# Splitting eight small reads between two DMA queues and moving one inverse root on VectorE

## The reference

```python
q = l2_normalize(qkv[..., :A_KEY_W].reshape(bsz, s, A_HEADS, A_DK)) * (A_DK ** -0.5)
a_mat = jnp.where(strict, jnp.einsum("bhncd,bhnsd->bhncs", k_beta, k) * decay, 0.0)
sol = lax.linalg.triangular_solve(a_mat + jnp.eye(CHUNK, dtype=f32), rhs, left_side=True, lower=True, unit_diagonal=True)
```

## Time and profile before

| | us |
|---|---|
| median of 3 runs | 952.58 |
| lowest, highest | 951.58, 954.92 |
| the profiled execution's own time | 954.44 |
| its span, first to last instruction | 952.6 |
| PE busy, of the span | 925.1 (97%) |
| DVE busy | 610.0 (64%) |
| ACT busy | 497.1 (52%) |

### The profile page before, as it was taken

One profiled execution on the slowest core, in us unless ns is written; L12 is line 12 of the kernel. 1 busy time (PEld: TensorE's weight loads), 2 busy tenths in 40 slices (PEclk: granted clock), 3 DMA queues, 4 the chain that ended last, 5 costly groups with the idle time before them and its releaser, 6 DMA issues.

```text
span 952.6 us, 13974 instructions
## 1 busy us (share of the span) xinstructions
PE 925.1 (97%) x5264; PEld 786.6 (83%) x5264; DVE 610.0 (64%) x1037; ACT 497.1 (52%) x867; POOL 31.1 (3%) x43
## 2 busy tenths in 40 slices
PE   5999989999999999899999999999999999999998
PEld 5899989799989898677888888887776788888886
DVE  4787967776566687867654454546887665554443
ACT  4478342464566576666544444535586654444431
POOL 1001000000000012100000000010000000000000
PEclk9999989999999999999999999999999999999999
DMA  9454331356533545314555655555444266555550
GB/s 327 139 174 145 96 104 45 111 183 218 175 134 133 162 146 196 110 45 133 178 176 178 191 192 188 177 177 174 140 132 134 92 198 191 181 176 179 183 190 22
DMA packets 106293, 148.22 MB, mean 156 GB/s; under 512 B 12564, under 2 KB 59344, under 8 KB 106112
## 3 DMA queue, kind: packets, MB, share of 16 engines
q1 hardware_dynamic: 102014, 145.34, 47.2%
q0 software_dynamic: 704, 1.77, 0.5%
q10 hardware_dynamic: 3522, 0.39, 0.3%
HBM read 146.03 MB, written 1.45 MB: 155 GB/s over the span
## 4 chain that ended last, share of the span: by engine, by line
PE 87%; DVE 7%; ACT 3%; issue 1%; DMA 1%; ACTq 0%; SPq 0%; DVEq 0%
PE ps L1879 25%; PE ps L1881 24%; PE ps L1880 24%; PE ps L1974 4%; DVE wlo L1159 3%; ACT whi L641 1%; PE ps L2111 1%; PE ps L2105 1%; PE ps L2259 1%; DVE G L1324 1%; PE ps L2467 0%; PE ps L2498 0%; DMA C<-in_consts 0%; PE ps L2046 0%; PE ps L2065 0%
## 5 line engine op out<-in xcount | busy, mean ns | idle before, releaser
L1159 DVE TENSOR_TENSOR wlo<-raw,whi 128x1024 fp32r<-128x1024 f32 (+1 forms) x272 | 321.3, 1222 | 213.4 <-ACT whi L641 213.1
L641 ACT ACTIVATE whi<-raw 128x1024 fp32r<-128x1024 f32 (+1 forms) x272 | 271.2, 1045 | 270.9 <-PE ps L1881 270.7
L1879 PE MATMUL ps<-whi,xh 128*128 128x512 f32 (+1 forms) x544 | 217.7, 400 | 1.3 <-DVE wlo L1159 1.0
L1881 PE MATMUL ps<-whi,xl 128*128 128x512 f32 (+1 forms) x544 | 211.9, 389 | 0.0
L1880 PE MATMUL ps<-wlo,xh 128*128 128x512 f32 (+1 forms) x544 | 211.5, 389 | 0.0
L1879 PEld LDWEIGHTS ps<-whi,xh 128*128 128x128 f32 x544 | 102.2, 188 | 23.1 <-issue 3.4
L1881 PEld LDWEIGHTS ps<-whi,xl 128*128 128x128 f32 x544 | 102.1, 188 | 21.4
L1880 PEld LDWEIGHTS ps<-wlo,xh 128*128 128x128 f32 x544 | 102.4, 188 | 18.6
L1879 PE MATMUL ps<-xh,whi 128*128 128x256 f32 x384 | 112.5, 293 | 3.3 <-DVE xl L1225 3.0
L1880 PE MATMUL ps<-xl,whi 128*128 128x256 f32 x384 | 109.6, 285 | 0.0
L1881 PE MATMUL ps<-xh,wlo 128*128 128x256 f32 x384 | 109.5, 285 | 0.0
(11 more groups left out here) (391 smaller groups left out, 1178.1 us busy)
## 6 DMA issues: line engine op xcount, KB each, us to landing
raw<-in_l_w_gate SPq DMA_DIRECT2D x44, 512.0 KB, 3.9
raw<-in_l_w_up SPq DMA_DIRECT2D x44, 512.0 KB, 4.9
raw<-in_l_w_down SPq DMA_DIRECT2D x44, 512.0 KB, 4.6
raw<-in_l_w_in SPq DMA_DIRECT2D x36, 512.0 KB, 4.5
raw<-in_a_w_in SPq DMA_DIRECT2D x32, 512.0 KB, 4.7
raw<-in_w_kv SPq DMA_DIRECT2D x16, 512.0 KB, 4.9
raw<-in_b_w_in SPq DMA_DIRECT2D x16, 512.0 KB, 4.4
raw<-in_l_w_o SPq DMA_DIRECT2D x16, 512.0 KB, 4.3
```

The costliest lines, as they stand in the source:

```text
L641: nc.scalar.activation(whi[:, g % HIGH, a], raw[:, g % RAW, a], ACT.Copy).then_inc(hi_done, 1)
L1159: nc.vector.tensor_tensor(wlo[:, g % LOW, a], raw[:, g % RAW, a], whi[:, g % HIGH, a].bitcast(F32), ALU.subtract).then_inc(lo_done, 1)
L1879: mm(o_, a_h, b_h, start=start, stop=False, skip_group_check=True)
L1881: return mm(o_, a_l, b_h, start=False, stop=stop, skip_group_check=True)
```

## The change

Two edits. On DVE the inverse root of the queries and its scaling move out of slot 43 into the first level of the joining, between the masks of the second and third quarters. The PSUM read stays in slot 43. The keys' root stays where it was. On the Y side SP issues four of the eight reads, and ACT the other four, in slot 54 (`CONV_V - 1`), behind the same waits as SP. The number of DMAs and the counts on `blocks` stay the same.

```diff
                     with nc.allow_non_contiguous_dma(reason="diagonal blocks of 16 by 16"):
-                        for b in range(NB):
+                        for b in range(NB // 2):
                             sp.dma_start(diagonal_block(Y, b), blocks_y[b].rearrange("n i j -> i n j")).then_inc(S("blocks"), 16)
...
+                if s == CONV_V - 1:
+                    act.wait_ge(S("inv_zero"), 2)
+                    act.wait_ge(S("blocks"), 16 * NB + 32)
+                    with nc.allow_non_contiguous_dma(reason="diagonal blocks of 16 by 16"):
+                        for b in range(NB // 2, NB):
+                            act.dma_start(diagonal_block(xn[:].rearrange("p t n -> p (t n)"), b),
+                                          blocks_y[b].rearrange("n i j -> i n j")).then_inc(S("blocks"), 16)
                 if s == CONV_V:
                     act.wait_ge(S("solved"), 1)
                     act.dma_start(blocks_x.rearrange("b n i j -> (b n) (i j)"), blk_x).then_inc(S("x_blocks"), 16)
...
             def summed(name, n):
 
-                ms, y, t = rms[name]
                 dve.wait_ge(S("col_sum"), n + 1)
-                nc.vector.tensor_scalar(by_stat(ms), stat_ps, 1.0, EPS, ALU.mult, ALU.add).then_inc(S("stat_read"), 1)
+                nc.vector.tensor_scalar(by_stat(rms[name][0]), stat_ps, 1.0, EPS, ALU.mult, ALU.add).then_inc(S("stat_read"), 1)
+
+            def rooted(name, n):
+
                 dve.wait_ge(S("stat_read"), n + 1)
-                inverse_root(ms, y, t).then_inc(step(name, "root"), 1)
+                inverse_root(*rms[name]).then_inc(step(name, "root"), 1)
                 dve.wait_ge(*past(name, "root", 1))
...
                 if s == COL_SUM_AT[0]:
                     summed("k", 0)
+                    rooted("k", 0)
...
                 if s == COL_SUM_AT[1] + 2:
                     summed("q", 1)
-                    link(nc.vector.tensor_scalar(rq, rq, float(P) ** -0.5, None, ALU.mult))
...
             for lv in range(3):
                 for q_ in range(4):
                     a = slice(512 * q_, 512 * q_ + 512)
+                    if lv == 0 and q_ == 2:
+                        rooted("q", 1)
+                        link(nc.vector.tensor_scalar(rq, rq, float(P) ** -0.5, None, ALU.mult))
                     dve.wait_ge(S("t2"), 4 * lv + q_ + 1)
```

## The result

The changed kernel took 956.38 us in the median of 20 runs (955.0 to 960.0), the kernel before 952.71 us in the median of 20 (951.58 to 955.36). The ratio is 1.0037, with a 95% interval of 1.0029 to 1.0045: slower by 3.5 us, by the ratio. The forecast was that nothing changes, 952.6 us with a range up to 955.4, and the measured time lies above that range. Rival B, given 8%, had said 956.7 us.

The account below looks back on a forecast made before the run. PE was taken to be bound by the chain through ACT's eight X-read issues and the silu, not by the Y reads. The terms 0 + 0 + 0 + 0 + 0 gave 0 us: 952.6 us, range 950.4 to 955.4.

Parts of the forecast that it names:

- Rival B: The blocks_x write stands behind the weight loads: 2.8 us later plus 1.3 us of clock, together 4.1 us, 956.7 us; chance 8%.
- The write of `blocks_x`: ACT's write, issued at 118.69 without slack, now behind 1 MB of weights: delay between 0 and 2.8 us, taken as 0.
- rival A: PE's clock stays up in t2, 1.8 us, and its 1.53 us gap goes: 949.3 us; chance 6%, clock alone 6%.
- the low part of unit 12: On DVE, without the root in slot 43, it runs 1.8 us earlier, from about 100.5; no gain in itself.
- that of unit 13: On DVE, unit 13's low part can start at 106.2 instead of 106.84, limited by its first high half.
- the solve's end: The rest of the solve comes 0.6 us earlier, L529 at 114.4 instead of 115.00; worth 0.
- ACT's four issues in its idle time: ACT's four added reads in slot 54 run from 116.2 to about 118.1, within its 5.18 us idle; cost 0.
- the loads at 118.13: SP's weight transfers, issued at 120.65 before, go out at about 118.1 after four fewer reads; gain 0.
- `t2` at 120.31: PE starts t2 at 120.5 as the Y reads land sooner and the 1.53 us wait goes; gain 0.
- the new gap behind its first quarter: PE's gap moves behind t2's first quarter, ended by the L809 copies at 123.16; later work starts as before, gain 0.
- the root hidden under PE's wait: The root's 2.3 us on DVE fit in its 4.38 us wait before the third quarter's mask; cost 0.
- Rival C: ACT's new issues overrun slot 54 if two queues double the 0.48 us issue: 1.4 us later, 954.0 us; chance 5%.

Follow-up runs that it names:

- just_behind: Changed kernel, with SP waiting for ACT's first L809 copy before issuing unit 17's weight loads; 953.59 us, ratio 1.0002 to the kernel before.
- split_only: Changed kernel with the queries' root and its scaling back in slot 43, leaving only the split of the Y reads; 956.01 us, ratio 1.0036 to the kernel before.
- reads_behind_write: Changed kernel with ACT's four Y reads issued right behind the blocks_x write instead of ahead of it; 955.47 us, ratio 1.0028 to the kernel before.
- half_loads: Changed kernel with only the first 512 KB of unit 17's weights ahead of the blocks_x write, the second load awaiting its landing; 955.38 us, ratio 1.0027.
- loads_held: Changed kernel, with SP waiting for the blocks_x write to land before issuing unit 17's weight loads; 952.47 us, ratio 1.0001 to the kernel before.
- root_only: Kernel before with only the root moved, SP issuing all eight Y reads; 953.67 us against 953.81, ratio 1.0005.
- write_first: Changed kernel with the blocks_x write moved from slot 55 to slot 54, ahead of ACT's four Y reads; 952.46 us, ratio 0.9999 to the kernel before.
- x_early: Kernel before, root moved, blocks_x write and four X reads in slot 54: 0.9979; variants with root in slot 43: 0.9977, or unit 15's high part later: 0.9966.

## Why the prediction was wrong

**The step that failed is "The write of `blocks_x`".** It took 0 for a delay that it had bounded by 0 and 2.8 us; it measured 2.4 us, of which 2.3 us reached the silu. The place, the absence of slack and the upper bound were right, and so was the mechanism of rival B. What was wrong was the choice between the bounds. It rested on the earlier trace rows: loads fill the engines only 1.8 us behind their issue, so a write issued 0.6 us behind them, with 0.8 us of its own to its bytes, would be through first. The 1.8 us are the time to full traffic, not to the first packet. The loads' first packet runs 1.09 us behind their issue, in the kernel before too (121.74 for 120.65). A write issued 0.56 us behind them has its own first packet due 0.56 + 0.86 = 1.42 us behind their issue, so the loads were on the engines first. The runs show the edge to lie near the order of issue: 0.38 us behind the write the loads do no harm (just_behind), 0.17 us ahead of it they cost 1.8 us (split_only). The nearest row was L526, 4.6 us to land behind a pair of loads. I had set it aside because it stood in the same queue as the loads; the write on the other queue took 4.2 us, nearly the same. For two ends that far apart the row that it was nearest to should have been taken: 2.8 us, giving 955.4 us before the clock.

The profile of the kernel before also had a row on the other queue, which the prediction did not use. ACT's eight X reads go out from 120.57, around and behind the loads that SP issues from 120.65:

```profile
G<-blocks_x ACTq DMA_DIRECT2D x8, 16.0 KB, 4.5
```

The first, issued ahead of the loads, landed in 2.6 us, the three issued from 121 to 122 us in 5.2 us (the median). With the loads issued long before, in the changed kernel, such a read takes 1.9 us. So the argument against rival B "that it is another queue" could have been met from the kernel before alone.

**The Trainium skill's rule on turns between the queues** (DMA: Bandwidth & Descriptors, "Queues, rings and completion order"), by which the delay would be a fraction of the 2.8 us, isn't borne out for the time ahead of the write's first packet: ACT's queue moved no packet from 120.5 to 121.5 while SP's moved 127, and the delay was 2.4 of 2.8 us. Once the write's packets ran, both queues moved packets in the same half microseconds (35 beside 87, then 90 beside 65). The measurement decides. The Trainium skill's other rule (same page, "Issuing engines are not separate DMA queues"), that a second issuing queue saves only the sequencer's time of issue, agrees with the case: SP was spared four issues of 0.48 us, and the Y reads landed in 1.8 us (SP's, median) and 2.0 us (ACT's) against 1.8 before. SP spent the time saved on issuing something harmful.

**The clock was mis-sized with it.** Rival B priced another 1.3 us for it; the trace shows 0.8 us. 2.3 + 0.8 = 3.1 us against the 4.1 us of rival B. The 956.7 us of rival B lies close to the 956.38 us measured partly by luck: the trace's stretch gives 952.7 + 3.1 = 955.8 us. The 0.4 us between that and the 3.5 us of the ratio are not accounted for; they lie within its interval (2.8 to 4.3 us).

Two traces are also not two medians. Each execution has a mean granted clock on record. It is 0.993 to 0.996 in all 42 executions of the four kernels whose write landed late (the changed one, split_only, reads_behind_write, half_loads), but in only 19 of the 77 of the kernel before that were timed beside the experiments; the rest are at 0.998 to 1.000. In every profiled execution 0.996 or less goes with 1.2 GHz in this stretch, and 0.998 or more with 2.4 GHz. So the kernel before loses the clock in some executions and the late write goes with its loss in all, and its profiled execution was one that had lost it (0.996, 954.44 us). What the low clock costs when nothing else changes is the 17.65 us of before against the 16.1 us of loads_held: 1.5 us, where rival A had worked out 1.8.

**The steps that held**, each with its number on the clock of before: the low part of unit 12 1.8 us earlier (102.33 to 100.51), that of unit 13 at 106.29 (106.2), the solve's end 0.5 us earlier where 0.6 was said (L529 at 114.50), the reads from 116.28 (116.2), ACT's four issues in its idle time (ACT's first L809 on time, 5.18 us idle as before), the loads at 118.13 (118.1), `t2` at 120.31 (120.5), the new gap behind its first quarter (1.85 us, ended by L809), the root hidden under PE's wait (root_only: 1.0005). So the gain was 0 as worked out, and root_only, loads_held and write_first, all within 0.05% of the kernel before with intervals of about 0.1% either way, bear it out for each part by itself. Rival A, the clock staying up and the gap gone, did not come in the changed kernel. Rival C, slower issues on two queues at once, is out: ACT's four took 1.87 us, SP's 1.80 us.

## What to carry to other kernels

When a queue is relieved of small transfers, look at what stands behind them: the next thing it issues comes earlier by just as much, and if that is large, it can overtake a small transfer that another queue is about to send. In these runs a small transfer that a chain waits for had to be issued ahead of the bulk, and 0.38 us ahead was enough; hold the bulk, or send the small one as soon as its data is there. And a wait on PE is worth only what separates its end from that of the next wait behind it: here 1.53 us of wait gave nothing, and 1.5 us taken out of ACT's chain, for which PE's wait was 0.65 us, gave 2 us by the ratio, a part of it through the clock.

## What the runs showed of the hardware that was not expected

- A write of 128 KB on ACT's queue, issued 0.17 to 0.57 us behind 1 MB of loads on SP's queue, took 3.6 to 4.2 us to land; issued 0.38 us or more ahead of them it took 1.7 to 1.9 us, whatever followed. Behind 512 KB it took 3.5 us. Whether it is held where the transfers are prepared or in the engines themselves was not told apart.
- From the issue to the first packet it was 0.85 to 0.89 us for that write and 1.03 to 1.10 us for the loads, and about another 0.8 us until the loads moved 359 GB/s (the kernel before, 121.74 and 122.5 us).
- ACT's DMA issues run ahead of activations that stand before them in its program. In the kernel before the first L819 goes out at 120.57, while the last L809 copies that stand ahead of it run only from 122.54. The silu, which stands behind the issues, starts at 124.51, when the last of them is out at 124.46.
- PE's clock in the first level: in single profiles it fell to 1.2 GHz in the kernels before, root_only and just_behind and in the four whose write landed late, and stayed at 2.4 GHz in loads_held, write_first and the three x_early kernels. In loads_held and write_first the idle times of PE are almost those of just_behind, and the stretch is 16.1 us in place of 17.7. The clocks of the executions show that it differs from one to the next: 0.996 or less in 5 of 12 of root_only, 7 of 10 of just_behind, 4 of 12 each of loads_held and write_first, and 2 of 31 of the three x_early kernels. What decides it stays open.
